# GpSimd takes the last conv group, and three steps change their place in the queues (Trainium2, one core)

## What is computed

```python
z = n @ w_in                      # q, k, v, glu, g_att, g_conv
o = _diff_attention(q, k, v, lam, cid)          # 8 heads, two softmax maps each, chunk mask
y_att = _rms(o, subln_w) * (1.0 - lambda_init)
u = glu[..., :CONV_CH] * jax.nn.sigmoid(glu[..., CONV_CH:])
u = _causal_dwconv(u, conv_dw_w, conv_dw_b)     # depthwise, 31 taps per feature
u = jax.nn.silu(_layernorm(u, conv_ln_w, conv_ln_b))
y_conv = u @ w_conv_out
m = jax.nn.sigmoid(g_att) * y_att + jax.nn.sigmoid(g_conv) * y_conv
h = h + m @ w_out                 # then a gated feed-forward with a 3-tap conv
...
x = x + rmsnorm(conv_ffn(h, ...), norm_ffn_post)   # the last step of the second block
```

## Time and profile before

| | |
|---|---|
| median of three runs | 1564.23 us |
| profiled execution | 1564.73 us, span 1562.9 us |
| PE busy | 1532.4 us, 98% of the span |
| DVE / ACT / POOL busy | 72% / 43% / 2% |
| mean granted TensorE clock | 0.996 |
| chain that ended last | PE 77%, DVE 15%, ACT 6% |

### The profile page before, as it was taken

How to read it: one execution, slowest core, us unless ns; L and a number is a source line. 1 busy time by engine, 2 the same in 40 slices (tenths; PEclk the granted TensorE clock), 3 DMA queues, 4 the chain that set the end, 5 groups by cost and what they waited for, 6 DMA issues and landing times.

```text
span 1562.9 us, 25443 instructions
## 1 busy us (share of the span) xinstructions
PE 1532.4 (98%) x9972; PEld 1368.4 (88%) x9972; DVE 1126.0 (72%) x1590; ACT 665.2 (43%) x1035; POOL 35.3 (2%) x66
## 2 busy tenths in 40 slices
PE   7999999999999999999999999999999999999998
PEld 7998988898999999999988888878788888888887
DVE  5899888888655577777774548897748988787123
ACT  5223455556662443334333344753646432333112
POOL 0000000100000000000000001000000000000000
PEclk9999999999999999999999999999999999999999
DMA  6323222222223333232223243322122233232321
GB/s 176 82 81 91 72 55 55 55 73 64 68 68 103 87 86 103 81 106 82 77 70 108 77 121 87 81 54 68 55 82 81 81 107 106 82 107 94 108 81 54
DMA packets 235295, 131.63 MB, mean 84 GB/s; under 512 B 20921, under 2 KB 228677, under 8 KB 235221
## 3 DMA queue, kind: packets, MB, share of 16 engines
q1 hardware_dynamic: 234836, 130.40, 29.7%
q0 software_dynamic: 384, 0.20, 0.1%
HBM read 128.48 MB, written 2.10 MB: 84 GB/s over the span
## 4 chain that ended last, share of the span: by engine, by line
PE 77%; DVE 15%; ACT 6%; issue 1%; DMA 0%; DVEq 0%; ACTq 0%
PE psP L677 25%; PE psS L677 22%; PE psP L742 8%; DVE conv L2059 7%; PE psS L1353 4%; PE psP L1353 4%; PE psP L699 4%; PE psP L1044 3%; DVE wl L1956 2%; PE psP L1221 1%; ACT prob L1512 1%; PE psS L1221 1%; ACT wh L1405 1%; PE psP L805 1%; DVE stat L2093 1%
## 5 line engine op out<-in xcount | busy, mean ns | idle before, releaser
L1956 DVE TENSOR_TENSOR wl<-raw,wh 128x2048 fp32r<-128x2048 f32 x124 | 284.1, 2291 | 178.3 <-ACT wh L1405 176.5
L677 PE MATMUL psP<-xh,wh 128*128 128x258 f32 (+2 forms) x1296 | 320.3, 312 | 13.8 <-ACT qkv L1499 8.9
L1405 ACT ACTIVATE wh<-raw 128x2048 fp32r<-128x2048 f32 x124 | 237.2, 1913 | 209.5 <-PE psS L1353 74.3
L677 PE MATMUL psP<-xh,wl 128*128 128x258 f32 (+2 forms) x1296 | 315.9, 308 | 0.0
L677 PE MATMUL psP<-xl,wh 128*128 128x258 f32 (+2 forms) x1296 | 315.3, 308 | 0.0
L677 PEld LDWEIGHTS psP<-xh,wh 128*128 128x128 f32 x1296 | 211.8, 191 | 30.3 <-issue 8.0
L677 PEld LDWEIGHTS psP<-xl,wh 128*128 128x128 f32 x1296 | 211.3, 190 | 12.0 <-issue 0.2
L677 PEld LDWEIGHTS psP<-xh,wl 128*128 128x128 f32 x1296 | 211.2, 190 | 11.9
L677 PE MATMUL psS<-xh,wh 128*128 128x258 f32 (+2 forms) x768 | 186.7, 307 | 0.4 <-DVE hT L1985 0.4
L677 PE MATMUL psS<-xh,wl 128*128 128x258 f32 (+2 forms) x768 | 185.9, 307 | 0.0
L677 PE MATMUL psS<-xl,wh 128*128 128x258 f32 (+2 forms) x768 | 185.6, 306 | 0.0
(11 more groups left out here) (463 smaller groups left out, 2440.1 us busy)
## 6 DMA issues: line engine op xcount, KB each, us to landing
raw<-in_w_in_dram SPq DMA_DIRECT2D x76, 512.0 KB, 5.0
raw<-in_w_up_dram SPq DMA_DIRECT2D x44, 512.0 KB, 4.9
raw<-in_ffn_up_dram SPq DMA_DIRECT2D x44, 512.0 KB, 5.0
raw<-in_ffn_down_dram SPq DMA_DIRECT2D x22, 512.0 KB, 4.1
raw<-in_w_out_dram SPq DMA_DIRECT2D x16, 512.0 KB, 4.7
raw<-in_w_down_dram SPq DMA_DIRECT2D x16, 384.0 KB, 3.6
raw<-in_w_down_dram SPq DMA_DIRECT2D x16, 320.0 KB, 4.0
raw<-in_w_conv_out_dram SPq DMA_DIRECT2D x8, 512.0 KB, 4.6
```

The costliest lines, as they stand in the source:

```text
L677: ins = mm(ps[0:rows, a, 0:nn], W[:, s, half, k, 0:rows], Y[:, k, c0 + a * nn:c0 + (a + 1) * nn], start=(k == 0 and p == 0), stop=(k == KT ...
L1405: fn(wh[:, n % 2], raw[:, n % 2], ACT.Copy).then_inc(s_hi, 1)
L1956: V.tensor_tensor(wl[:, n % 2], raw[:, n % 2], wh[:, n % 2].bitcast(f32), ALU.subtract).then_inc(s_lo, 1)
```

## The change

Four edits. POOL computes all 30 taps of group 7, five after each of heads 0 to 5: each tap is a multiply by the tap weight into `nf[:, 0]` and an add into `conv[:, 7]`, with a semaphore wait behind each. DVE has 210 taps left, 14 in step 0 and 18 a step after, and gets one new step in step 8, `last_group`, which adds group 7 to `csum` behind `lo(n+1)`. On ACT the scaling of the head outputs (`scale_heads`) moves from ahead of `empty(h, 1)` to behind `copy_probs(a, 1)`, ahead of `exps(a, 3)`. On DVE in step 0, `lo(n+2)` moves from the end of the step to behind the first tap. At the end, `residual(2, 2)` on PE moves between the two halves of the last tile, and DVE weighs the second half of the last tile behind the output of tile 2.

```diff
@@ -334,6 +334,7 @@
         s_ex = sem("exps_ready")
         s_cb = sem("probs_combined")
         s_mp = sem("meta_probs_gathered")
+        s_gt7 = sem("last_group_taps")
         s_vrp = sem("meta_values_repeated")
         s_at = sem("attention_transposed")
         s_ac = sem("attention_copied")
@@ -624,6 +625,15 @@
                 for t in range(TT):
                     pool.wait_ge(s_cb, 4 * a + t + 1)
                     pool.tensor_copy(pm[:, t, 0:NM], prob[:, PO[t]:PO[t] + NM]).then_inc(s_mp, 1)
+                if a == 0:
+                    pool.wait_ge(s_ft, NH)
+                for k in range(1 + 5 * a, min(6 + 5 * a, CK)):
+                    if k > 1:
+                        pool.wait_ge(s_gt7, 2 * k - 2)
+                    w = cdw[:, NH * k + NH - 1:NH * k + NH]
+                    pool.tensor_scalar(nf[:, 0, 0:T3], u[:, NH - 1, C3 + k:C3 + k + T3], w, None, ALU.mult).then_inc(s_gt7, 1)
+                    pool.wait_ge(s_gt7, 2 * k - 1)
+                    pool.tensor_tensor(conv[:, NH - 1, :], nf[:, 0, 0:T3], conv[:, NH - 1, :], ALU.add).then_inc(s_gt7, 1)
 
             pool.wait_ge(s_sqf, 4)
             pool.memset(wab[:], 0.0).then_inc(s_pz, 1)
@@ -1378,13 +1388,14 @@
             pe.wait_ge(s_lo, n + c + 1)
             pe.wait_ge(s_pl, CREDIT + FG + 2 * c + 2)
             for t in range(TT):
-                for half in range(2):
-                    down_tokens(c, (half,), (t,)).then_inc(s_dn, 1)
+                down_tokens(c, (0,), (t,)).then_inc(s_dn, 1)
+                if t == 3:
+                    pe.wait_ge(s_dw, 6)
+                    residual(2, 2)
+                down_tokens(c, (1,), (t,)).then_inc(s_dn, 1)
                 if 0 < t < 3:
                     pe.wait_ge(s_dw, 2 * t)
                     residual(t - 1, t - 1)
-            pe.wait_ge(s_dw, 6)
-            residual(2, 2)
             pe.wait_ge(s_oc, 2)
             residual(3, 0)
 
@@ -1485,7 +1496,7 @@
                 act.wait_ge(s_mm, gi + 1)
                 if h >= NH:
                     g = 4 * (h - NH) + q
-                    act.wait_ge(s_cv, g + 1)
+                    act.wait_ge(*((s_cv, g + 1) if g < NH - 1 else (s_gt7, 2 * (CK - 1))))
                     dst, width, func, scale = sgc[:, g, 0:T3], H3, ACT.Tanh, 0.5
                 elif q == 3:
                     dst, width, func, scale = yT[:, h, C3:T], H3, ACT.Tanh, 0.5
@@ -1548,6 +1559,8 @@
                 if b == NH - 1:
                     root(1, psP[1], H3, eps5)
                 nc.scalar.preload_act_table(ACT.Exp)
+
+            def scale_heads(b):
                 act.wait_ge(s_or, b + 1)
                 for t in range(TT):
                     fn(otok[:, t, :], otok[:, t, :], ACT.Copy, scale=var[:, 0, t:t + 1])
@@ -1589,6 +1602,9 @@
                     copy_probs(a, 1)
                     if h == NH:
                         centred_squares(4, 6)
+                if b >= 0:
+                    scale_heads(b)
+                if 0 <= a < NH:
                     exps(a, 3)
                 hi(n + 2)
                 if h == NH:
@@ -2047,7 +2063,7 @@
 
             def taps(count):
 
-                for j in range(tap[0], min(tap[0] + count, NH * (CK - 1))):
+                for j in range(tap[0], min(tap[0] + count, (NH - 1) * (CK - 1))):
                     g, k = divmod(j, CK - 1)
                     k += 1
                     w = cdw[:, NH * k + g:NH * k + g + 1]
@@ -2064,7 +2080,12 @@
                             if g > 1:
                                 dve.wait_ge(s_cs, g - 1)
                             V.tensor_tensor(csum, conv[:, 0, :] if g == 1 else csum, y, ALU.add).then_inc(s_cs, 1)
-                tap[0] = min(tap[0] + count, NH * (CK - 1))
+                tap[0] = min(tap[0] + count, (NH - 1) * (CK - 1))
+
+            def last_group():
+                dve.wait_ge(s_gt7, 2 * (CK - 1))
+                dve.wait_ge(s_cs, NH - 2)
+                V.tensor_tensor(csum, csum, conv[:, NH - 1, :], ALU.add).then_inc(s_cs, 1)
 
             def glu(n):
                 if n:
@@ -2147,7 +2168,12 @@
                     combine(a, 0)
                     combine(a, 1)
                 lo(n + 1)
-                taps(4 if h else 8)
+                if h == NH:
+                    last_group()
+                taps(4 if h else 1)
+                if h == 0:
+                    lo(n + 2)
+                    taps(5)
                 if h == NH:
                     clear_sums()
                 if b >= 0:
@@ -2164,7 +2190,7 @@
                     combine(a, 2)
                 if h == NH:
                     centred(4, 6)
-                taps(5)
+                taps(3)
                 if 0 <= a < NH:
                     maxima(a, 3)
                 taps(3)
@@ -2177,13 +2203,14 @@
                     inverse(1, T3)
                     for k in range(KT):
                         V.tensor_tensor(conv[:, k, :], conv[:, k, :], rstd[:, 0:T3], ALU.mult).then_inc(s_ln, 1)
-                lo(n + 2)
+                if h:
+                    lo(n + 2)
                 if h == NH:
                     add_square(8 + KT - 1, T3)
-                taps(7 if h else 1)
+                taps(6 if h else 0)
                 if h == NH + 1:
                     gated(NH - 1, psS[0])
-            assert tap[0] == NH * (CK - 1)
+            assert tap[0] == (NH - 1) * (CK - 1)
             for k in range(KT):
                 dve.wait_ge(s_nh, 8 + k + 1)
                 V.tensor_tensor(xl[:, k, C3:T], conv[:, k, :], xh[:, k, C3:T].bitcast(f32), ALU.subtract).then_inc(s_nl, 1)
@@ -2633,8 +2660,8 @@
                 lo(N_DN2 + c)
             dve.wait_ge(s_wp, 16)
 
-            def weigh(t):
-                for half in range(2):
+            def weigh(t, halves=range(2)):
+                for half in halves:
                     c = slice(512 * half, 512 * (half + 1))
                     dve.wait_ge(s_dq, 2 * t + half + 1)
                     V.tensor_tensor(xo[:, t, c], ALLP[t][:, half, :], wpost[:, c], ALU.mult).then_inc(s_dw, 1)
@@ -2654,8 +2681,9 @@
             token_output(0, 0)
             weigh(2)
             token_output(1, 1)
-            weigh(3)
+            weigh(3, (0,))
             token_output(2, 2)
+            weigh(3, (1,))
             token_output(3, 0)
```

## The result

The changed kernel takes 1580.28 us, the median of four runs (1579.25 to 1580.52). The kernel before, on the same chip, takes 1563.51 us (four runs). The ratio is 1.0104, with a 95% interval of 1.0092 to 1.0116: 16.8 us slower. I had said 1558 us, in a range that ends at 1573. The profiled execution has a span of 1578.3 us where before it had 1562.9.

A forecast was written before the change was run, and what follows sets the result against it. Two loops of nearly one length, DVE's and PE's, share the head stage; relieving DVE pays until PE binds. 4.9 to 6.9, + 3.9, - 3.7, + 0.6, say 6.5 us gained: 1558 us, range 1553 to 1573.

The forecast's parts named there:

- I take the row that is there, near 0: DVE beside POOL's taps: delay taken near 0, bounds 0 to some 4.1 us a step, below 1.4 hidden under PE.
- my first rival: DVE is blocked as long as POOL reads: DVE loop 36.5 us a step, 1571.5 us in all; chance 0.26.
- with no POOL work: Step 7 with DVE blocked by POOL's reads: 7 taps less, PE's 33.8 us, giving back 0.9 of its 34.7.
- POOL's pair: One tap on POOL, multiply 0.5 and add 1.0: 2.0 to 2.9 us with waits; five, behind the split, 12 to 17.
- my third rival: POOL is late: at 4 us a pair PE waits for `vr` in six steps, 35 us more, about 1592; chance 0.04.
- The relieved steps: Steps 3 to 7: 33.8 us a step, set by PE; offload and later scaling together gain 3.9 us.
- The stall moved: Step 1: PE stalls some 3 us before its third part, waiting for ACT's emptying near 158.5, with a low clock behind.
- Step 8: The last add behind `lo(n+1)` makes PE wait before the means: 2.1 us lost plus 1.6 of low clock, 3.7.
- The end: Last tile: PE 0.87 later, but the last pair of adds starts near 1558.4 instead of 1559.05, 0.6 us gained.
- The later scaling: ACT in the head stage: emptying ends near 267.7, PE's wait of 1.01 us goes, at no cost.
- The early split: Step 0 on DVE: step 2 starts 1.7 us earlier with a low clock, 3.7 without; 4.9 to 6.9 through step 2.
- the rest of step 2: Step 2 on PE: the 1.90 us stall and the 1.6 of low clock behind it go, counted as 1.6 + 1.6.

The follow-up runs named there:

- the kernel with memsets: Changed kernel with each of POOL's 30 taps replaced by five chained memsets of 516 columns, which read nothing: 1559.32 us.
- the gap kernels: Changed kernel, POOL cut to one tap in each of steps 1 to 6, during DVE's wait: 1561.41 us; with step 0's split back at its end: 1559.04.

## Why the prediction was wrong, step by step

**The step that failed** is "I take the row that is there, near 0", the delay of DVE beside POOL's taps. The row showed taps beside `pm` copies, whose reads are over at once; it could not speak of 516 elements. Without POOL's reads the change gains 1564.18 - 1559.47 = 4.7 us; with them it loses 16.1 to 16.8. So the reads are worth some 21 us. Of these the adds alone cost 1573.96 - 1559.32 = 14.6; the multiplies alone cost nothing, and the other 6 appear only when both are there, as I take it since the adds have then used up the time that DVE had to spare. Over the whole run DVE's taps are late by 203 x (865 - 756) ns = 22.1 us and its splits by 124 x (2333 - 2291) ns = 5.2, together 27.3 us, more than the 23.7 that left it.

**The mechanism was that of my first rival**, to which I gave 0.26, and the Trainium skill (SBUF — State Buffer, Who interferes with whom) had stated it. The trace before showed one direction, these runs show both: the split stretches POOL's multiply to 3.66 us, and POOL's add stretches a tap to 1.79. That the later one waits for the whole of the first, as the skill has it, the trace bears out for the add (328.31 against 328.29), but not for the multiply: it lasts 1.57 us, and a tap beside it is late by 0.43 at most. I gave "no row shows it" more weight than "the same pair of engines excludes itself the other way round", though the mirror of that row was the better evidence.

**The rival's size was off too**: 1571.5 for 1580. Three terms of it, against the earlier trace rows and the fourth parts. A step with POOL's taps takes (354.17 - 206.02) / 4 = 37.0 us in place of 36.5: 2.2 more in four steps. Step 7 takes 37.95, where I had written 33.8 "with no POOL work": head 5's taps start at 353.78, just ahead of the fourth part of step 6, and all lie inside this interval. That alone is 4.1 us, a slip in counting which interval the work falls into. And step 2 kept 1.1 of its gain instead of 1.9. Together 7.1. Another 0.8 is that I took 34.7 to 34.8 us for a step before, which holds for three of the five; all five take 172.9, or 34.6 each.

**POOL's pair.** Multiply 1.57 us at the least for my 0.5, add 1.27 for my 1.0, and five pairs took 316.08 to 336.65 = 20.6 us of my 12 to 17, so `vr` was late, as my third rival had it. But its price, 35 us, was not paid: with DVE behind, PE's waits are one and the same time under other names. The select over 4 partitions was no measure for a multiply by a tap weight. The Trainium skill (GPSIMD Engine Reference, Performance versus the Vector engine) led to an estimate of 1.1 us for the add; the trace has 1.27. What the same page says of one input, "roughly line-rate" (Engine selection), does not come out of the trace at this length: 1.57 us for 516 elements is longer than the add, though it blocks DVE for less. With one length only, no run here tells a slow rate from a fixed cost.

**What was right.** The relieved steps, where nothing delays DVE: 33.75 us measured for 33.8, and 172.92 - 168.73 = 4.2 gained in steps 3 to 7 for my 3.9. The stall moved ahead of the transposes, 2.94 us idle at 158.47, predicted near 158.5 and 3 long, with a low clock behind it. Step 8: 3.4 for 3.7. The end: the last square moved 0.87 behind PE as I took it (1570.57 to 1572.91 in the changed kernel, 1554.55 to 1556.02 before, as distances 2.34 and 1.47), and from the square before it to the last pair of adds it is 3.86 us for 4.50, 0.64 gained for 0.6. The later scaling alone gives 0; with DVE relieved the waits ahead of the third parts are gone, but no run takes its share apart.

**What was mis-sized without deciding the result.** The early split with the rest of step 2 gained 207.13 - 203.32 = 3.8, for 4.9 to 6.9. Step 2 gave its part, 3.4 for 3.2; the split gave 170.65 - 170.28 = 0.4 up to the fourth part of step 1, where I had 1.7 with a low clock. In the profile of the kernel with memsets the same part starts at 166.62, 4.0 earlier, where I had 3.7 at full clock. And the gap kernels show that in another balance the early split costs 2.4.

## What to carry to other kernels

Before work goes to POOL, ask what DVE reads at that moment: POOL's reads of SBUF and DVE's instructions with two SBUF inputs take turns, so a POOL add of 516 elements costs DVE about as much (0.7 to 1.04 us) as the tap it takes off it (0.79). Work on POOL pays where DVE waits: one pair a step in its 3 us gap is worth 3.6 us, and with the later scaling and the new order at the end 5.0 us are gained over the kernel before. And a row shows the absence of a delay only for work of its own length.

## What the runs showed of the hardware that was not expected

A multiply with one SBUF input and a scalar for each partition takes 1.57 us on POOL for 516 elements, more than the add with two inputs (1.27), but delays a DVE tap by 0.43 us at most, where the add delays it by 0.7 to 1.04. So the time that DVE loses is not the duration of POOL's instruction.

The same idle stretches of PE do not always lower the clock. The kernel without POOL's taps and the one with memsets have the same stall of 2.9 us near 157 us; behind it one profile shows

```profile
155.00:166.00 11.00, 8.06 (x42) 6.94 (x41) 9.29 (x15) 4.99 (x13) 0.66 (x1) 0.69 0.12 28
```

and the other

```profile
155.00:166.00 11.00, 8.06 (x67) 7.47 (x65) 9.29 (x16) 5.69 (x14) 0.66 (x1) 1.00 0.03 7
```

with the granted clock at 0.69 and at 1.00. The first execution took 1560.09 us, the second 1555.28, and the kernel of the second has other executions up to 1560.20. Behind the 2.7 us idle ahead of the means it is the same: the clock of the first is at 0.53 there, that of the second at 1.00. And in the changed kernel 1.80 us idle at 198 has a low clock behind it, 1.79 at 235 has none. What decides between them no run here shows. I had read the earlier trace rows as if a stall of such a length always lowered the clock; one of 2.9 us can leave it up.
